# Joining the high-part products of a float32 matmul split in two parts: gate, up, the late experts' chunks and the experts' chunks 16 to 35

## The reference

```python
def peer_ffn(h, w_query, sub_keys, expert_u, expert_v):     # 16384 experts, 8 heads x 16 chosen
    ...
    gate = jax.nn.softmax(best, axis=-1)
    act = jax.nn.gelu(jnp.einsum('thkd,td->thk', expert_u[experts], hb), approximate=False)
    return jnp.einsum('thk,thkd->td', gate * act, expert_v[experts])

h = h + 0.5 * swiglu(rmsnorm(h, ffn1_norm[i]), ffn1_w_gate[i], ffn1_w_up[i], ffn1_w_down[i])
...                                                          # a mixer with a convolution and a state space part
h = h + 0.5 * swiglu(rmsnorm(h, ffn2_norm[i]), ffn2_w_gate[i], ffn2_w_up[i], ffn2_w_down[i])
```

## Time and profile before

| | |
|---|---|
| runs | 1738.68, 1740.67, 1740.92 us, median 1740.67 us |
| profiled execution | span 1738.2 us from the first to the last instruction (the profile has no other time for it; the median of the runs is 2.5 us more) |
| instructions | 29000 |
| mean granted TensorE clock | 0.983 of full speed |
| mean DMA rate | 183 GB/s, 318.52 MB |
| ScalarE, GpSimd busy | 907.9 us (52%), 83.8 us (5%) |

### The profile page before, as it was taken

The page is one execution under the profiler, slowest core; times in us unless marked ns, Lnnn a source line. Parts: engine busy times, 40 slices in busy tenths (PEclk is TensorE's granted clock), DMA queues, the critical chain, the costliest instruction groups (busy, mean ns, idle before and its releaser), DMA issues.

```text
span 1738.2 us, 29000 instructions
## 1 busy us (share of the span) xinstructions
PE 1647.9 (95%) x11512; PEld 1479.5 (85%) x11512; DVE 1250.9 (72%) x2028; ACT 907.9 (52%) x1192; POOL 83.8 (5%) x50
## 2 busy tenths in 40 slices
PE   6898788999999999999999999999998989999997
PEld 6776668998999888789999999899998777899996
DVE  5886666899988899986666655655557787655556
ACT  4354555554555555455444445544446766644446
POOL 1100003522000000000000000000000000000000
PEclk9898999999999999999999999999999999999999
DMA  6644233446565455566555565454554533555551
GB/s 264 274 168 157 97 118 137 155 161 206 189 202 188 170 207 192 207 218 249 203 211 216 195 214 187 150 204 177 194 173 155 203 137 121 200 194 174 193 191 73
DMA packets 53418, 318.52 MB, mean 183 GB/s; under 512 B 5953, under 2 KB 6113, under 8 KB 19362
## 3 DMA queue, kind: packets, MB, share of 16 engines
q1 hardware_dynamic: 52098, 310.60, 50.2%
q0 software_dynamic: 1184, 6.05, 0.9%
HBM read 307.17 MB, written 9.47 MB: 182 GB/s over the span
## 4 chain that ended last, share of the span: by engine, by line
PE 73%; DVE 18%; ACT 6%; issue 1%; DMA 1%; SPq 0%; DVEq 0%; ACTq 0%
PE pb L870 73%; DVE w_lo L1851 4%; DVE ar L1851 4%; ACT ar L1410 3%; DVE ar L1863 2%; ACT w_hi L1410 2%; DVE ar L2215 1%; DMA raw<-in_wall 1%; DVE ar L2013 1%; DVE ar L2212 1%; DVE raw L2013 1%; ACT L1410 1%; DVE ar L2010 1%; DVE ar L2219 1%; DVE sm L2078 0%
## 5 line engine op out<-in xcount | busy, mean ns | idle before, releaser
L1851 DVE TENSOR_TENSOR w_lo<-raw,w_hi 128x1024 fp32r<-128x1024 f32 x467 | 572.2, 1225 | 253.2 <-ACT w_hi L1410 227.7
L870 PE MATMUL pb<-HX,w_hi 128*128 128x256 f32 x3904 | 715.8, 285 | 13.0 <-DVE w_lo L1851 6.0
L1410 ACT ACTIVATE w_hi<-raw 128x1024 fp32r<-128x1024 f32 x498 | 528.3, 1061 | 299.3 <-PE pb L870 278.3
L870 PEld LDWEIGHTS pb<-HX,w_hi 128*128 128x128 f32 x3904 | 613.8, 193 | 20.1 <-DVE w_lo L1851 5.2
L870 PE MATMUL pb<-HX,w_lo 128*128 128x256 f32 x1952 | 553.7, 284 | 0.0
L870 PE MATMUL pb<-w_hi,HC 128*128 128x512 f32 (+1 forms) x1648 | 526.3, 391 | 4.2 <-DVE HC L1863 3.3
L870 PEld LDWEIGHTS pb<-HX,w_lo 128*128 128x128 f32 x1952 | 376.0, 193 | 0.0
L870 PEld LDWEIGHTS pb<-w_hi,HC 128*128 128x128 f32 x1648 | 309.6, 188 | 68.6 <-DVE HC L1863 2.7
L870 PE MATMUL pb<-w_lo,HC 128*128 128x512 f32 (+1 forms) x824 | 320.6, 389 | 0.0
L1851 DVE TENSOR_TENSOR ar<-ar 128x512 bf16<-128x512 bf16 (+8 forms) x470 | 247.7, 564 | 53.2 <-ACT ar L1410 33.5
L1410 ACT ACTIVATE ar<-pb 128x512 f32<-128x512 f32 (+3 forms) x200 | 112.4, 562 | 256.5 <-PE pb L870 155.4
(11 more groups left out here) (148 smaller groups left out, 705.5 us busy)
## 6 DMA issues: line engine op xcount, KB each, us to landing
raw<-in_wall SPq DMA_DIRECT2D x257, 1024.0 KB, 4.8
ar<-in_wmod SPq DMA_DIRECT2D x24, 512.0 KB, 3.7
act_keep<-ar SPq DMA_DIRECT2D x28, 256.0 KB, 5.6
ar<-act_keep SPq DMA_DIRECT2D x28, 256.0 KB, 5.1
x<-in_wmod SPq DMA_DIRECT2D x8, 512.0 KB, 5.3
ar<-in_bigrows POOLq DMA_DIRECT2D x2, 1024.0 KB, 5.3
ar<-acs_keep POOLq DMA_DIRECT2D x2, 1024.0 KB, 8.2
ar<-in_crow SPq DMA_DIRECT2D x2, 512.0 KB, 6.0
```

What stands on the lines that cost most here:

```text
L870: return e.matmul(o, l, r, start=start, stop=stop, skip_group_check=True)
L1410: a.did(e.activation(out, in_, func, scale=scale, **kw), sig)
L1851: v.did(e.tensor_tensor(out, a_, b_, op), sig)
```

## The change

Chunks 16 to 63 of u, gate and up get `feat_pair` in place of `feat_half`: the high part of the weights meets the high and the low part of the activations in one matmul of 512 columns (two runs of 256, `HX[:, :, k, :]`), 8 of them, and then the low part meets the high part in 8 of 256 columns. The result of a half is 128x512 in a bank of its own: columns 0 to 255 and 256 to 511 have still to be added. So a chunk needs a pair of banks. ScalarE copies the second 256 columns of each half to SBUF (`u_parts`), VectorE adds them to the first (`u_sum`), and gelu reads SBUF. The high products wait for `w_hi` alone, the low ones for `w_lo`.

```diff
+PAIR0 = 16
+        PB = [... range(2)];  P23, P45, P67: pairs of banks [128, 2, 512]
+        def u_bank(c):
+            return P45 if c >= NU or c % 2 else P23
+            def feat_pair(u, out, j=None):
+                hi, lo = parts(u, "p (k n) -> p k n", k=8)
+                t.wait_ge(s_hi, ORD[u] + 1)
+                for k in range(8):
+                    if j is not None:
+                        t.wait_ge(s_nl, both_turned(j, k))
+                    mm(out, hi[:, k, :], HX[:, :, k, :], k == 0, k == 7)
+                t.wait_ge(*LOW[u])
+                for k in range(8):
+                    ins = mm(out[:, 0:256], lo[:, k, :], HX[:, 0, k, :], False, k == 7)
+                t.did(ins, s_used)
             def u_half(c, m):
+                if c >= PAIR0:
+                    if c == PAIR0 + 1:
+                        t.wait_ge(s_gelu, c - 2 + m)
+                    elif c > NU:
+                        t.wait_ge(s_sum, u_summed(c - 1))
+                    elif c > PAIR0 + 1:
+                        t.wait_ge(s_sum, u_summed(c - 2))
+                    feat_pair(PEER_U[c] + m, u_bank(c)[:, m, :])
+                    return
...
ScalarE:
+            def u_parts(c):
+                for m in range(2):
+                    a.wait_ge(s_used, used(PEER_U[c] + m))
+                    if c > PAIR0:
+                        a.wait_ge(s_sum, u_summed(c - 1))
+                    act(apart[:, m, :], u_bank(c)[:, m, 256:512], ACT.Copy, sig=s_part)
             def gelu(c):
+                if c >= PAIR0:
+                    a.wait_ge(s_sum, u_summed(c))
+                    act(act_made(c), act_made(c), ACT.Gelu, sig=s_gelu)
+                    return
...
                 if h % 2:
-                    gelu(c)
+                    if c >= PAIR0:
+                        u_parts(c)
+                    else:
+                        gelu(c)
+                elif c > PAIR0:
+                    gelu(c - 1)
                 for b in blocks_after(h):
                     g_copy(b)
...
+            gelu(NU - 1)                                  # ahead of the loop over v
...
VectorE:
+            def u_sum(c):
+                v.wait_ge(s_part, u_part(c, 1))
+                if KEPT[10] <= c < NU:
+                    v.wait_ge(s_ao, kept(c - 4))
+                tt(act_made(c).rearrange("p (m t) -> p m t", m=2), u_bank(c)[:, :, 0:256], apart, ADD, sig=s_sum)
                 ahead(U_PEER + h)
+                if h % 2 == 0 and h // 2 > PAIR0:
+                    u_sum(h // 2 - 1)
+            u_sum(NU - 1)                                 # ahead of one_hots(NBL + 3)
...
                 if NU <= c + 2 < 64:
+                    u_sum(c + 2)                          # ahead of weigh(c + 2)
```

```diff
-                    tt(f_full, f_sg[:, c % 2, :], PB[BK[c % 2][1]][:, :], MUL, sig=s_mf)
+                    for m in mid_parts(c):
+                        v.wait_ge(s_part, ffn_part(n0, c, 1, m.stop - 1))
+                        tt(full[:, m, :], P67[:, m, 0:256], f_upart[:, m, :], ADD, sig=s_sum if m.stop == 2 else None)
+                        v.wait_ge(s_sg, n0 + c + 1)
+                        tt(full[:, m, :], full[:, m, :], sg[:, m, :], MUL, sig=s_mf)
```

More of the change, by code:

```diff
@@ L392, in sem @@
             return es.enter_context(nc.semaphore(name))
-        PB = [es.enter_context(nc.psum_tensor(f"pb{i}", [128, 512], F32)) for i in range(8)]
+        PB = [es.enter_context(nc.psum_tensor(f"pb{i}", [128, 512], F32)) for i in range(2)]
+        P23, P45, P67 = [es.enter_context(nc.psum_tensor(f"pb{n}", [128, 2, 512], F32)) for n in ("23", "45", "67")]
+        PB += [p[:, i, :] for p in (P23, P45, P67) for i in range(2)]
         raw = sb("raw", NRAW, CH)
@@ L410, in program @@
         fsc = sb("fsc", 3, 256)
-        AW = 26000
+        AW = 26176
         ar = sb("ar", AW)
@@ L498, in program @@
         s_sg, s_mf, s_mh, s_ml = sem("s_sg"), sem("s_mf"), sem("s_mh"), sem("s_ml")
+        s_part, s_sum = sem("s_part"), sem("s_sum")
         s_dwh, s_dw, s_xb, s_dt, s_an, s_dta = (
@@ L662, in program @@
         act3 = fsc.rearrange("p a b -> p (a b)")[:, 0:512]
+        apart = a3.get(2, 256)
         act1f = act1.rearrange("p a b -> p (a b)")
@@ L690, in program, with u_part, u_summed, ffn_part @@
         f_mid = WR
-        BK = [(4, 5), (6, 7)]
+        f_gpart, f_upart = a7.get(2, 256), a7.get(2, 256)
+        def u_bank(c):
+            return P45 if c >= NU or c % 2 else P23
+        def u_part(c, m):
+            return 2 * (c - PAIR0) + m + 1
+        def u_summed(c):
+            return c - PAIR0 + 1
+        def ffn_part(n0, c, p, m):
+            return 2 * (64 - PAIR0) + 4 * (n0 + c) + 2 * p + m + 1
+        def ffn_summed(n0, c, p):
+            return 64 - PAIR0 + 2 * (n0 + c) + p + 1
+        def mid_parts(c):
+            return [slice(0, 2)] if c < 10 else [slice(0, 1), slice(1, 2)]
+        def mid_made(n0, c, m):
+            return n0 + n0 // 11 + c + 1 + (m if c == 10 else 0)
         a8 = Arena()
@@ L1233, in mids @@
                 def mids(c, m, i):
-                    t.wait_ge(s_ml, n0 + c + 1)
+                    t.wait_ge(s_ml, mid_made(n0, c, m))
                     a_ = m * 256 + i * 128
@@ L1238, in gate_up @@
                 def gate_up(c):
[L1239 to L1240 removed]
                     at = ffn_at(base, c)
                     for p in range(2):
+                        if c:
+                            t.wait_ge(s_sum, ffn_summed(n0, c - 1, p))
                         for m in range(2):
[L1244 to L1245 removed]
+                            feat_pair(at[p] + m, (P67 if p else P45)[:, m, :], j if c == p == m == 0 else None)
                         if c == p == 0:
@@ L1689, in scalar_program @@
                         ahead(PEER_U[c + 2] + m)
-                    a.wait_ge(s_w, c + 1)
+                    u_parts(c + 2)
                     gelu(c + 2)
@@ L1706, in gate_up @@
                     at = ffn_at(base, c)
[L1707 to L1710, removed]
+                    ahead(at[0])
+                    a.wait_ge(s_used, used(at[0]))
+                    act(f_gpart[:, 0, :], P45[:, 0, 256:512], ACT.Copy, sig=s_part)
+                    ahead(at[0] + 1)
+                    a.wait_ge(s_used, used(at[0] + 1))
+                    act(f_gpart[:, 1, :], P45[:, 1, 256:512], ACT.Copy, sig=s_part)
+                    ahead(at[1])
                     a.wait_ge(s_gr, n0 + c + 1)
                     act(f_sg[:, c % 2, :], f_sg[:, c % 2, :], ACT.Silu, sig=s_sg)
-                    a.wait_ge(s_mf, n0 + c + 1)
+                    ahead(at[1] + 1)
+                    for m in range(2):
+                        a.wait_ge(s_used, used(at[1] + m))
+                        act(f_upart[:, m, :], P67[:, m, 256:512], ACT.Copy, sig=s_part)
                     if c > 1:
                         a.wait_ge(s_used, used(ffn_at(base, c - 2)[2] + 1))
-                    act(f_mid[:, c % 2, 0, :], f_full, ACT.Copy, sig=s_mh)
+                    for m in mid_parts(c):
+                        s_ = slice(m.start * 256, m.stop * 256)
+                        a.wait_ge(s_mf, mid_made(n0, c, m.start))
+                        act(f_mid[:, c % 2, 0, s_], f_full[:, s_], ACT.Copy, sig=s_mh)
                 gate_up(0)
@@ L2348, in vector_program @@
                         ahead(PEER_U[c + 2] + m)
+                if NU <= c + 2 < 64:
+                    u_sum(c + 2)
                 if c + 2 < 64:
@@ L2371, in gate_up @@
                         inverse_rows(2 if n0 else 0)
-                    v.wait_ge(s_used, used(at[0] + 1))
-                    tt(f_sg[:, c % 2, :].rearrange("p (m t) -> p m t", m=2),
-                       PB[BK[c % 2][0]][:, :].rearrange("p (m t) -> p m t", m=2), bc(inv, 1, 2), MUL, sig=s_gr)
+                    sg = f_sg[:, c % 2, :].rearrange("p (m t) -> p m t", m=2)
+                    v.wait_ge(s_part, ffn_part(n0, c, 0, 1))
+                    tt(sg, P45[:, :, 0:256], f_gpart, ADD, sig=s_sum)
+                    tt(sg, sg, bc(inv, 1, 2), MUL, sig=s_gr)
                     for m in range(2):
                         ahead(at[1] + m)
-                    v.wait_ge(s_sg, n0 + c + 1)
-                    v.wait_ge(s_used, used(at[1] + 1))
-                    tt(f_full, f_sg[:, c % 2, :], PB[BK[c % 2][1]][:, :], MUL, sig=s_mf)
-                    v.wait_ge(s_mh, n0 + c + 1)
-                    tt(f_mid[:, c % 2, 1, :], f_full, f_mid[:, c % 2, 0, :].bitcast(F32), SUB, sig=s_ml)
+                    full = f_full.rearrange("p (m t) -> p m t", m=2)
+                    for m in mid_parts(c):
+                        v.wait_ge(s_part, ffn_part(n0, c, 1, m.stop - 1))
+                        tt(full[:, m, :], P67[:, m, 0:256], f_upart[:, m, :], ADD, sig=s_sum if m.stop == 2 else None)
+                        v.wait_ge(s_sg, n0 + c + 1)
+                        tt(full[:, m, :], full[:, m, :], sg[:, m, :], MUL, sig=s_mf)
+                    for m in mid_parts(c):
```

(3 more changed lines are left out.)

2 lines of the change are left out of this document (removed).

## The result

| | before | after |
|---|---|---|
| median of the runs, us | 1739.7 (1738.3 to 1740.9, 4 runs) | 1747.4 (1745.4 to 1749.6, 4 runs) |
| ratio to before, 95% interval | | 1.0045 (1.0031 to 1.0060) |
| span of the profiled execution, us | 1738.2 | 1743.7 |

The medians, ranges and numbers of runs in this document leave out two slow executions at a low granted clock, one of E2 (2496 us at 0.60) and one of E8 (2679 us at 0.56).

What follows compares the result with a forecast made beforehand. VectorE was taken to bound 433 to 764 us, TensorE 780 to 1110 and the feed-forwards; 18.2 - 6.0 - 9.4 + 0.4 = +3.2 us gave a span of 1741.4, plus 2.5 a median of 1744, range 1729 to 1751.

Steps and rivals of the forecast that it cites:

- The ring: Gates' matrix stage: sum, gelu, block copy, high part, low part wait in a loop; 8.14 us a pair, before 7.38.
- rival (a): Gates' matrix stage: only VectorE's own work binds, not the loop through ScalarE; 7.97 us a pair, 1732.5 us; chance 0.20.
- The shift of the value stage: Value stage, from about 580 to 764 us: starts 18.2 us late and passes that on whole to TensorE's following chain.
- the walk: Passage from sum(33) to the second weighing's low part, both engines followed operation by operation: 15.5 us, ending at 597.6.
- TensorE's saving in the chunks: Chunks 16 to 35: joining 40 halves would save TensorE 4.3 us, all lost in waits.
- The joined product at 226.7 ns: TensorE: a 512-column matmul of two runs takes 226.7 ns against 240 for two; 0.107 us saved a half.
- late experts: Chunks 36 to 63: joining 56 halves saves TensorE 6.0 us.
- Rival (c): TensorE: a joined matmul with two runs costs as much as two, nothing is saved; 1759 us; chance 0.08.
- The feed-forwards: Both feed-forward parts: joining 88 halves saves 9.4 us, less 0.2 each for low products behind the last normalised row.
- both at zero: Late experts and feed-forwards: added copies and sums cost nothing; if cover failed, the last chunk up to 1 us each part.
- The late experts' cover: Late experts' stage: VectorE has 121 us free of 330 and gets 22; TensorE has 5.4 us of work after a sum.

Runs made afterwards that it cites:

- E2: Changed kernel with gelu(c-1) moved one half later on ScalarE, behind the odd half's weight copy; 1735.2 us, ratio to before 0.9980.
- E8: Changed kernel with joined products beside the gates' matrix from chunk 26 instead of 16; 1735.9 us, ratio to before 0.9985.
- E9: Changed kernel, chunks 16 to 35 joined but without copies and sums, gelu reading the first 256 columns from PSUM; 1724.3 us, ratio to before 0.9915.
- E4: Changed kernel with the activations' high and low parts stored beside each other for each k, one run of 512 columns; 1747.0 us, ratio to before 1.0045.
- E6: Changed kernel, chunks 16 to 35 as before; feed-forwards (except first parts) make two halves' 16 joined products, then 16 low ones; 1730.4 us, ratio to before 0.9955.
- E7: Changed kernel with only the feed-forwards joined, chunks 16 to 35 and late experts as before; 1734.7 us, ratio to before 0.9976.
- E5: Changed kernel, chunks 16 to 35 as before, half 62's weight copy and low part between activation halves in feed-forwards' last chunk; 1728.1 us, ratio 0.9938.
- E3: Changed kernel with the sums of chunks 16 to 35 on GpSimd, ScalarE copying both parts out of PSUM; 1741.1 us, ratio to before 1.0014.

## Why the prediction was right, and its misses

- **The ring** was the step that carried the forecast, and it held. Worked out 8.14 us a full pair, measured 8.21 (495.41 to 503.62, and 510.22 to 518.42); without the even block 7.41 and 7.51; without the odd one 6.67 and 6.60 to 6.88; 17 pairs 132.5 and 133.6. ScalarE's way of 2.53 us was 2.56. E2 shows the cause, by opening it: rival (a)'s 7.97 us a pair is what VectorE needs alone (8.01), but not what this kernel takes.
- **The shift of the value stage** was forecast as 18.2 us and is 19.5 between marks: 1.1 more from the pairs, 0.3 from the walk. In the trace it reads 18.2 (780.87 against 762.68), because that execution was 1.3 us early before the stage. That the shift goes through the value stage unchanged held.
- **TensorE's saving in the chunks is lost in the waits**: held. E9 shows 3.1 us (4.1 by the medians) that stand ready; in E2, with the ring open, the pair is still 8.01 us, VectorE's, and none of it comes out.
- **The joined product at 226.7 ns** held in size: 227, but 232 for the first five of each run behind 256-column products. A half saves 0.092 to 0.097 us, not 0.107: late experts 5.4, not 6.0. Rival (c) is out. E4 and E6 place the 5 ns; why the chip does it stays open. The Trainium skill ("TensorE: Matmul & The Clock Gate", section "Back-to-back issue gap") gives the 2.5 ns of fixed cost for a matmul by itself; in this stream they don't hold for joined products either: 226.7 ns are 13.3 over the columns.
- **The feed-forwards** were the term that was mis-sized: -9.4 + 0.4 worked out, -5.6 measured (E7 alone: -4.1 by the medians). Between the blocks of down products a chunk saves 0.37 us (0.092 a half), 8.1 for 88 halves, so 1.3 went there. The first eight halves of a feed-forward give 0.5 us in the first and lose 0.24 in the second, where 0.73 were due: 0.2 and 1.0 lost to the rows that come k by k, against my 0.2 each. The last chunk's stretch is 0.62 us longer in each: I had written "both at zero", with up to 1 us if that cover failed. It failed in part. I had followed the activation's halves, which were in time, and not the weight copy that is queued behind them on ScalarE; E5 gives 0.4 back.
- **The late experts' cover** held: no wait of TensorE for a sum between 780 and 1110.

Sum of the change by the traces +8.5 against +3.2 forecast: 1.3 from the stage of the ring, 0.6 from the late experts, 3.4 from the feed-forwards. All three missed to the same side. That the time still lies within 3.4 us of 1744 owes 1 us to luck: the median that the forecast started from was 1 us above that of the four runs. In the span only 5.5 of it show, since the mixer was 1.9 and the start 1.3 us shorter in that execution.

## What to carry to other kernels

When work moves off the busiest engine, go round the engines before adding up their loads: here sum, gelu, high part and low part closed a loop of two in-order queues, and 11.3 of the 22.6 us that the new copies and sums cost hung on where one 0.63 us operation stood. The trade of TensorE for VectorE paid here in the stages where VectorE's row has room (the late experts, the feed-forwards) and not beside the gates' matrix, so decide on it stage by stage. Behind a split into halves, follow what is queued after them too.

## What the runs showed of the hardware

- A GpSimd add that reads SBUF holds up VectorE's SBUF operations: in each of the 20 adds of E3 one VectorE operation took 0.9 to 1.1 us longer (a one-hot of 0.42 us took 1.41), and that is more than the 0.79 us it was spared.
- Products of 512 columns come every 227 ns, but the first five behind a run of 256-column ones every 229 to 236, 232 in the mean (after, E4, E6).
- The granted clock stayed at 1.00 through 13 of TensorE's 14 waits, and fell at the passage to the value stage, during the last and longest of them, 3.9 us. Windows of the changed kernel (stretch, its us, busy us of PE, PEld, DVE, ACT, POOL, clock, DMA share, GB/s):

```profile
500.00:560.00 60.00, 55.07 (x540) 48.26 (x540) 51.81 (x89) 35.05 (x52) 0.00 (x0) 1.00 0.49 170
582.00:598.00 16.00, 12.09 (x112) 10.45 (x113) 11.76 (x19) 10.02 (x15) 0.00 (x0) 0.80 0.47 165
```

  0.80 lies between the two levels, 2.4 GHz (1.00) and 1.2 GHz (0.50). E4 has 0.89 in 582 to 598, and its stage is as long as that of after to 0.1 us; so no cost of the deeper fall shows there, where VectorE and ScalarE set the pace.
